# An MLP in fp32 of split products: norm scale, gain and squared ReLU on other engines, and plain first blocks

## The reference

```python
def rmsnorm(x, g):
    xf = x.astype(F32)
    y = xf * lax.rsqrt(jnp.mean(xf * xf, axis=-1, keepdims=True) + EPS)
    return (y * g.astype(F32)).astype(x.dtype)

def sq_relu_mlp(x, w_up, w_down):
    h = jax.nn.relu(x @ w_up)
    return (h * h) @ w_down
...
            x = x + o.astype(x.dtype) @ w_attn_out[j]
        x = x + sq_relu_mlp(rmsnorm(x, norm_ffn[l]), w_up[l], w_down[l])
```

## Time and profile before

| what | value |
|---|---|
| median of 3 runs | 2617.59 us (2609.69 to 2621.41) |
| the profiled execution | 2625.56 us, span of its trace 2623.7 us |
| mean granted clock of TensorE, as a share of full speed | 0.954 |
| TensorE busy | 2402.5 us, 92% of the span |
| VectorE busy | 1687.5 us, 64% |
| ScalarE busy | 707.3 us, 27% |
| GpSimd busy | 605.5 us, 23% |
| DMA | 119.72 MB, mean 46 GB/s |

### The profile page before, as it was taken

How to read it: one execution, slowest core, us unless ns; L and a number is a source line. 1 busy time by engine, 2 the same in 40 slices (tenths; PEclk the granted TensorE clock), 3 DMA queues, 4 the chain that set the end, 5 groups by cost and what they waited for, 6 DMA issues and landing times. The chain is left out here.

```text
span 2623.7 us, 41047 instructions
## 1 busy us (share of the span) xinstructions
PE 2402.5 (92%) x16298; PEld 2278.2 (87%) x16298; DVE 1687.5 (64%) x2677; ACT 707.3 (27%) x1356; POOL 605.5 (23%) x446
## 2 busy tenths in 40 slices
PE   6899999977899999999998999997799999999998
PEld 6898888866899999989998877877799899998998
DVE  6555555577766666576676665567866666767664
ACT  3232222333121211211223353353112122121115
POOL 3000000125222222232222011027322222223223
PEclk7999999997899999999999999998899999999999
DMA  3112121110121111111111311100112111111121
GB/s 108 41 45 62 45 62 33 42 34 17 34 64 32 47 49 32 48 48 32 48 49 51 93 30 46 33 17 17 49 33 64 32 40 56 32 48 48 32 65 67
DMA packets 160983, 119.72 MB, mean 46 GB/s; under 512 B 23623, under 2 KB 140276, under 8 KB 160836
## 3 DMA queue, kind: packets, MB, share of 16 engines
q1 hardware_dynamic: 160724, 118.10, 15.3%
q10 hardware_dynamic: 144, 0.02, 0.0%
HBM read 110.94 MB, written 12.33 MB: 47 GB/s over the span
## 5 line engine op out<-in xcount | busy, mean ns | idle before, releaser
L2476 PE MATMUL acc<-h_hi,w_hi 128*128 128x352 f32 x1440 | 490.7, 341 | 89.5 <-DVE x_res L1488 84.4
L2478 PE MATMUL acc<-h_hi,w_lo 128*128 128x352 f32 x1440 | 481.0, 334 | 0.0
L2477 PE MATMUL acc<-h_lo,w_hi 128*128 128x352 f32 x1440 | 480.7, 334 | 0.0
L1488 DVE TENSOR_TENSOR x_res<-x_res,acc 128x1056 f32<-128x1056 f32 x240 | 299.8, 1249 | 170.6 <-PE acc L2478 170.6
L2476 PEld LDWEIGHTS acc<-h_hi,w_hi 128*128 128x128 f32 x1440 | 285.5, 198 | 107.6 <-DVE x_res L1488 95.1
L2477 PEld LDWEIGHTS acc<-h_lo,w_hi 128*128 128x128 f32 x1440 | 286.8, 199 | 0.0
L2478 PEld LDWEIGHTS acc<-h_hi,w_lo 128*128 128x128 f32 x1440 | 286.5, 199 | 0.0
L2426 PE MATMUL acc<-T_hi,w_hi 128*128 128x264 f32 x768 | 222.2, 289 | 23.0 <-DVE w_lo L1449 22.2
L2426 PE MATMUL acc<-op_hi,w_hi 128*128 128x264 f32 x768 | 219.7, 286 | 6.8 <-DVE w_lo L1449 6.2
L2427 PE MATMUL acc<-T_lo,w_hi 128*128 128x264 f32 x768 | 220.4, 287 | 0.0
L2428 PE MATMUL acc<-T_hi,w_lo 128*128 128x264 f32 x768 | 220.1, 287 | 0.0
(11 more groups left out here) (344 smaller groups left out, 5627.7 us busy)
## 6 DMA issues: line engine op xcount, KB each, us to landing
w_raw<-in_w_up SPq DMA_DIRECT2D x64, 512.0 KB
w_raw<-in_w_down SPq DMA_DIRECT2D x64, 512.0 KB
w_raw<-in_w_mlstm_in SPq DMA_DIRECT2D x24, 512.0 KB
x_in<-in_x_prompt SPq DMA_DIRECT2D x8, 512.0 KB, 3.8
w_raw<-in_w_mlstm_out SPq DMA_DIRECT2D x8, 512.0 KB
w_raw<-in_w_q SPq DMA_DIRECT2D x16, 256.0 KB
w_raw<-in_w_attn_out SPq DMA_DIRECT2D x16, 256.0 KB
out_y_prompt<-y_out SPq DMA_DIRECT2D x8, 512.0 KB, 2.7
```

The lines of the kernel that those rows point to most:

```text
L1488: V.tensor_tensor(blocks(x_res[:, k]), blocks(x_res[:, k]), row_banks(layer, k), ALU.add).then_inc(row_taken, 1)
L2476: T.matmul(out[:, b], hi[:, c], mh[:, span(b)], start=(c == 0), stop=False)
L2477: T.matmul(out[:, b], hi[:, c], ml[:, span(b)], start=False, stop=False)
L2478: x = T.matmul(out[:, b], lo[:, c], mh[:, span(b)], start=False, stop=(c == 1))
```

## The change

**In every block.** The gain's product goes from VectorE to ScalarE: `with_scale` makes it in 8 operations of 128x128 for each half of the weights, with the gain as the operation's scale. relu and square go to ScalarE too, as two operations in place (`squared_relu`). The product with rstd goes from GpSimd to VectorE (`scaled`), behind the square. The buffer h_scaled is gone. GpSimd keeps the four sums of weights, and waits for the new products with the gain. In the down part the two low halves of h move one row further back.

**At the entries.** The first two blocks of each layer (PLAIN = 2) have a plain up part: `tile` makes 128 rows of it from x_hi and x_lo, with 72 matmuls of 352 columns in three PSUM banks, two tiles a block. The rows of x_res are split into x_hi and x_lo without the gain (`prepare`), the weights in operations of 1024 columns (`plain_high`, `plain_low`). The sums T1 to T4 are made by VectorE, 4 operations of 528 columns each, and split beside the plain tiles (`t_sums_of`, `t_low`, on ScalarE `t_high`); T4 overwrites a part of x_hi and x_lo, and so is split only behind the last tile. B11, B21 and B22 are no longer separate copies: they are quarters of x_hi and x_lo. The sum over features is made within the first tile (`between`). GpSimd makes only the sums of squares there. The Winograd scheme begins with block 2, and the hardware loop with block 3.

The diff, cut to its core:

```diff
+            def with_scale(layer, f, s, i):
+
+
+                act.wait_ge(w_loaded[(s + i).parity], landed(s + i).value)
+                norm = (FFN0, FFN1)[layer]
+                for k in range(KD):
+                    g = gains[:, norm * KD + k:norm * KD + k + 1]
+                    x = nc.scalar.activation(raw(s + i, 8)[:, k], raw(s + i, 8)[:, k], ACT.Copy, scale=g)
+                x.then_inc(g_ready, 1)
...
+            def squared_relu(layer, f, c):
+
+                n = (f + NF * layer).times(2) + (2 - c)
+                if is_plain(f):
...
+                    nc.scalar.activation(blocks(z_of[c]), row_banks(layer, 1 - c), ACT.Relu).then_inc(tile_taken, 1)
+                    act.wait_ge(tile_taken, 4 * layer + 2 * f.const + 2 - c)
+                else:
...
+                    nc.scalar.activation(z_of[c], z_of[c], ACT.Relu).then_inc(relu_ready, 1)
+                    act.wait_ge(relu_ready, ((f + (LAYER_UPS * layer - PLAIN)).times(2) + (2 - c)).value)
+                nc.scalar.activation(z_of[c], z_of[c], ACT.Square).then_inc(sqr_ready, 1)
...
                 def down(f, s):
-                    if not static(f, NF - 1):
+                    if not (static(f, 0) or static(f, NF - 1)):
+                        squared_relu(layer, f + 1, 1)
+                        squared_relu(layer, f + 1, 0)
                         h_high(layer, f + 1, 1)
                         h_high(layer, f + 1, 0)
...
                     else:
+                        with_scale(layer, f + 2, s + 2, 0)
+                        with_scale(layer, f + 2, s + 2, 1)
                         for j in (0, 1, 3):
                             up_high(layer, f + 2, s + 2, j)
...
-            def scale(layer, f, c):
-
-                b = f + NF * layer
-                pool.wait_ge(z_dve, (b.times(7) + (7 - c)).value)
-                nc.gpsimd.tensor_tensor(h_scaled[:, f.parity, c], z_of(f)[c], rstd[:], ALU.mult).then_inc(tz_ready, 1)
-
...
-            def square_of_relu(layer, f, c):
-
-                dve.wait_ge(tz_ready, ((f + NF * layer).times(2) + (2 - c)).value)
-                z = z_of(f)[c]
-                V.scalar_tensor_tensor(z, z, 0.0, h_scaled[:, f.parity, c], ALU.max, ALU.mult).then_inc(zz_ready, 1)
+            def scaled(layer, f, c):
+
+                dve.wait_ge(sqr_ready, ((f + NF * layer).times(2) + (2 - c)).value)
+                if static(f, 0):
+                    dve.wait_ge(ms_ready, 2 + 2 * layer)
+                V.tensor_tensor(z_of[c], z_of[c], rstd[:], ALU.mult).then_inc(zz_ready, 1)
...
                     if static(f, 0):
-                        up_low(layer, f, s, 3)
+                        plain_low(layer, f, s, 1)
+                        t_sums_of(layer, "T1")
+                        t_low(layer, "T1")
+                        mean_square(1 + 2 * layer)
+                        plain_low(layer, f + 1, s + 2, 0)
+                        scaled(layer, f, 1)
+                        t_sums_of(layer, "T3")
+                        scaled(layer, f, 0)
+                        h_low(layer, f, 1)
+                        plain_low(layer, f + 1, s + 2, 1)
+                        h_low(layer, f, 0)
+                        return
...
+                        elif not static(f, NF - 1):
                             if k < 2:
-                                square_of_relu(layer, f + 1, 1 - k)
-                            if k in (1, 2):
-                                h_low(layer, f + 1, 2 - k)
+                                scaled(layer, f + 1, 1 - k)
+                            if k in (2, 3):
+                                h_low(layer, f + 1, 3 - k)
...
+                def tile(f, s, i):
+
+                    n = 2 * f.const + i
...
+                    for k in range(KD):
+                        if n == 0:
+                            pe.wait_ge(xl_ready, KD * no + k + 1)
+                        for b in range(TB):
+                            T.matmul(out[:, b], hi[:, k], x_hi[:, k, span(b)], start=(k == 0), stop=False)
+                            T.matmul(out[:, b], hi[:, k], x_lo[:, k, span(b)], start=False, stop=False)
+                            x = T.matmul(out[:, b], lo[:, k], x_hi[:, k, span(b)], start=False, stop=(k == KD - 1))
```

More of the change, by code:

```diff
@@ L842, in square @@
                 m = (FFN0, KV, FFN1).index(norm)
-                pair_of = (act_a, act_b) if norm == KV else (squares[:, 0], squares[:, 1])
                 act.wait_ge(x_final, final_count(norm, k))
@@ L914, in entry_row, with t_high @@
-            def entry_row(layer, r):
-                for name, j in ROW_ITEMS[r]:
-                    item_high(layer, name, j)
-                if r < 5:
-                    square((FFN0, FFN1)[layer], r)
+                if static(f, 1):
+                    act.wait_ge(tl_ready, 16 * layer + T_AT["T4", 3])
+                nc.scalar.activation(h_hi[:, f.parity, c], z_of[c], ACT.Copy).then_inc(hh_ready, 1)
+            def t_high(layer, name):
+                hi = operand(name)[0]
+                for j in range(4):
+                    act.wait_ge(t_sum, 16 * layer + T_AT[name, j])
+                    nc.scalar.activation(hi[:, j], t_sums[name][:, j], ACT.Copy).then_inc(th_ready, 1)
@@ new lines, in sum_chunks @@
+            def sum_chunks(m):
+                for k in range(1, KD):
+                    pool.wait_ge(chunk_squared, KD * m + k + 1)
+                    x = nc.gpsimd.tensor_tensor(rstd[:], (act_a if k == 1 else rstd)[:], (act_a, act_b)[k % 2][:], ALU.add)
+                    if k < KD - 1:
+                        x.then_inc(chunk_summed, 2 if k == 1 else 1)
+                        pool.wait_ge(chunk_summed, (KD - 1) * m + k + 1)
+                    else:
+                        x.then_inc(ssq_ready, 1)
@@ L1925, in up @@
+                    up_low(layer, f, s, 2)
+                    for j in (4, 5, 6):
+                        up_low(layer, f, s, j)
+                    combine(layer, f, "U2")
+                    combine(layer, f, "U3")
+                    end = layer == 1 and static(f, NF - 1)
+                    if end:
+                        last_split(s + 2, 0)
                     else:
                         down_low(layer, f + -1, s + 2, 0)
-                        for name in ("C11", "U4", "C22"):
-                            combine(layer, f, name)
@@ L1936, in up @@
+                    combine(layer, f, "C21")
+                    if not end:
                         down_low(layer, f + -1, s + 2, 2)
-                        combine(layer, f, "C12")
+                    combine(layer, f, "C12")
+                    if not end:
                         down_low(layer, f + -1, s + 2, 3)
```

592 lines of the change are left out of this document (262 added, 330 removed).

## The result

The changed kernel takes 2419.23 us (median of 4 runs, 2415.47 to 2423.57) against 2619.5 us for the kernel before: a ratio of 0.9241, with a 95% interval of 0.9211 to 0.9272. The forecast was 2420. The profiled execution takes 2420.09 us with a span of 2418.2, so 205.5 us less than the profiled one of before. TensorE is busy for 96% of the span; ScalarE's share has risen from 27% to 41%, GpSimd's fallen from 23% to 14%. The mean granted clock is 0.985 for 0.954.

A forecast was written before the change was run, and what follows sets the result against it. It took TensorE's waits for VectorE's late additions, held up by GpSimd, and the passages as the bound. Gains of 126.6 + 38 + 33 = 198 us from 2625.56 give 2428, less 8 for the median 2420; range 2395 to 2490.

The forecast's parts named there:

- The loops: The two MLP loops, 13 blocks each: TensorE's waits vanish, gaining 13 x 5.08 + 13 x 4.66 = 126.6 us.
- The chain: Start of each down part: ScalarE's relu and square, VectorE's rstd product, then the row 0 addition, done at 5.42 us.
- The margin before row 2: In the down part, addition 0 ends at 5.42 us and TensorE reaches row 2 at 5.77: 0.3 us spare.
- the floor of 43.35: Time of one MLP block if TensorE never waits: 20.30 us for the up part, 23.05 for the down part.
- The cause named for them: In the loops' down parts, VectorE's additions to x_res come late because its operations ahead of them wait for GpSimd.
- the two long operations: VectorE's product on act_b, 3.52 us, and low half of act_b, 2.34 us; both end 1.12 us after a GpSimd operation.
- The passages: Output projection's last rows to the first down part's end: 111 for 149.2 us and 121.7 for 154.6, gaining 38 and 33.
- The rest: Gates, mLSTM units, attention and the last down part keep their order; the last down part set at nothing, give or take 2.
- A late chain: Rival: ScalarE's chain before row 2 is s us longer, so every block waits s - 0.3; 2440 to 2505 us, chance 0.2.
- s = 2: Chain before row 2 longer by 2 us: 26 x (1.7 + 1.6) = 86 us lost, clock fall included, giving 2506 us.
- act_b's operations are slow of themselves: Rival: the act_b buffer is slow and GpSimd innocent; its product still takes 3.45 us, row 2 waits 1.9; 2530 us, chance 0.07.
- TensorE cannot hold 2.4 GHz through a block without a pause: Rival: in the loops the clock falls to 1.2 GHz for a share of work; slower from 18%, 2702 at a quarter; chance 0.03.

The follow-up runs named there:

- the late copies: Changed kernel plus unused copies of 1056 columns on ScalarE ahead of the loops' first relu; one costs 0.67 us a block, two 1.63, three 4.07.
- the kernel without them: Changed kernel with VectorE's first two sum-of-squares evacuations earlier, T4's low halves and the next up part's weight low halves later: 2401.97 us beside 2418.65.

## Why the prediction was right

**The loops, 126.6 us forecast, 124.4 measured.** The chain runs as reckoned: square of act_b done 2.93 us after the start (2.97 forecast), the product 4.22 (4.25), addition 0 5.39 (5.42), addition 1 7.72 (7.76), the low halves 8.89 and 11.26 (8.9 and 11.3). The margin before row 2, put at 0.3 us, is 0.3 by the late copies. The whole miss is the 0.08 us that each of 26 blocks takes over the floor of 43.35.

**The cause named for them was right in kind and half wrong in its weight.** GpSimd does hold VectorE up, as forecast, but the text put the two long operations side by side and let the norm product's departure stand first. By the runs that departure is worth 0.35 to 0.51 us of 4.42; what counts most is that the gain's product and the low half of act_b, held up by a sum of weights, no longer both stand ahead of addition 1. The sum came out right because it was made of places in queues, and not of this attribution.

**Who is held up.** The forecast let the low half of act_a wait for the first sum of weights and end at 12.6. It went the other way: VectorE's operation had begun 0.16 us earlier and kept its 1.25 us, and GpSimd's sum took 2.26 instead of 1.3. The loop's time does not hang on this, since the forecast's later end was covered too. The Trainium skill (SBUF — State Buffer, SBUF: two separate sides) says of a VectorE operation with two SBUF inputs and a GpSimd operation that reads SBUF that the one that "starts first gets the pair for the whole instruction; the other fully blocks", and the rows agree in both directions.

**The price of the gain on ScalarE.** Two operations of 129 columns in 0.63 us had stood for 2.5 us in each eight; eight take 2.44 and sixteen 4.78. The budget of the Trainium skill that would have made sixteen 6.5 (ScalarE: Activation LUTs, Rules for kernel authors) did not hold here: operations that follow each other start 0.29 us apart at 128 columns.

**The passages, 38 and 33 forecast, 43.2 and 31.1 measured.** Behind the last row 78.5 and 77.3 us were measured for 79.5; the stops are 3.08 and 2.03 us in layer 0, 1.88 and 2.03 in layer 1, for 3.3 and 2.0 forecast. The 1.5 us charged for the clock behind the second stop were not spent in this execution: it fell behind the first ones only. Up to the last row the two layers missed in opposite directions: 27.6 us for 31.5 in layer 0, since the pace of 3.75 us a row set in only with the later rows, and 46.3 for 42.2 in layer 1, where VectorE's work between rows was taken as hidden and TensorE waited 0.8 to 1.7 us at three places for its additions and 0.5 for another operand. Without the stops the text promised 20 us more, but its own terms for them (3.3, 1.7, 2 and 1.5 in each layer) make 17, and the kernel without them takes 16.7 less. Which part of the entry's change brings the passages' 74 us, the plain blocks, the sums on VectorE or the lighter load of GpSimd, no run takes apart; it is read from the stages.

**The rest, set at nothing,** shows 6.9 us, of which 3.5 are no more than runs of one code differ among themselves. That the median of 2419.23 us lies so close to 2420 is in part luck, since two misses of some 7 us cancel. The profiled execution gained 205.5 us and not 198. And the forecast took 8 us off for the distance of the profiled execution from the median, which is 0.9 us now.

**The rivals.** A late chain was the right one to fear: the margin is what it was said to be. Its price for s = 2 was too high, because the clock was let fall behind a wait of 1.7 us; at 1.63 us a block it costs only that, 26 x 1.63 = 42 us and not 86. That act_b's operations are slow of themselves, and that TensorE cannot hold 2.4 GHz through a block without a pause, are refuted by the product of 1.26 us and by two loops of 564.6 us at 1.00.

## What to carry to other kernels

Where one engine frees buffers for another, list what stands in its queue ahead of each freeing operation, and add up the ends against the consumer's pace: this gave the loops to 2%. An operation that an idle-looking engine lengthens costs only if it stands ahead of such an operation, so moving it behind that operation can be worth more than taking the other engine's work away. When a stop is removed, ask at once what is late next: here it took a second move to keep the gain of the first.

## What the runs showed of the hardware

A wait of TensorE of 1.46 us left its granted clock at 1.00 in every block, waits of 1.88 to 2.12 lowered it at some times and not at others, 2.44 us in 12 blocks of 13, 2.6 in 9 of 13 or 23 of 26; a fall costs 1.5 to 1.6 us of work. GpSimd's product of a tile of 1056 columns with itself takes 1.94 us, that of two tiles 2.5. They are recorded with 2.38 and 2.9 where a low half of weights on VectorE had begun 0.12 us before them, and so the 2.9 of the norm product before the change is itself in part a hold-up. VectorE's 240 additions with one input in PSUM take 1.24 to 1.26 us in all thirteen traces, whatever GpSimd does beside them.
